# Samples' weight panels: eight head-free ones put into the heads, and twelve multiplied as high and low parts in place of plain f32

## What is computed

```python
proj = rmsnorm(x, g_norm) @ w_in
u_p, z_p, q, k, v, z_r, gates = split(proj)           # u_p, z_p: 1024; q, k: 4 x 256; v, z_r: 4 x 512; gates: 2 x 1024
gate_p, gate_r = split(gates + b_gate)
pooled = multi_scale_pool(u_p, pool_buf)              # windows 2, 4, 8, 16, then a 256 x 256 matrix a group, times pool_scale
y_pool = (pooled * silu(z_p)) @ w_branch_pool
o, s_new = retention(rope(q), rope(k), v, ret_state)  # per head; s_new = decay * s + k^T v
y_ret  = (norm(o) * gn_ret * silu(z_r)) @ w_branch_ret
merged = sigmoid(gate_p) * y_pool + sigmoid(gate_r) * y_ret
out = rmsnorm(x + merged @ w_out, g_final)
```

## Time and profile before

| | us |
|---|---|
| runs | 3106.29, 3093.57, 3103.41; median 3103.41 |
| the profiled execution | 3093.96 |
| its span | 3092.4 |
| TensorE busy | 2985.6 (97%) |
| VectorE busy | 1832.8 (59%) |
| ScalarE busy | 1153.4 (37%) |
| HBM traffic | 188 GB/s over the span |

### The profile page before, as it was taken

How to read it: one execution, slowest core, us unless ns; L and a number is a source line. 1 busy time by engine, 2 the same in 40 slices (tenths; PEclk the granted TensorE clock), 3 DMA queues, 4 the chain that set the end, 5 groups by cost and what they waited for, 6 DMA issues and landing times.

```text
span 3092.4 us, 36008 instructions
## 1 busy us (share of the span) xinstructions
PE 2985.6 (97%) x13000; PEld 2299.2 (74%) x13000; DVE 1832.8 (59%) x2590; ACT 1153.4 (37%) x1892; POOL 709.0 (23%) x503
## 2 busy tenths in 40 slices
PE   6999999999999999999998999999999999999997
PEld 5888888888778888888887878778888878762222
DVE  7666566765454757566664575667567466744331
ACT  5434444445554434443433233333333333322110
POOL 4253534343332344433432000000000000001110
PEclk9999999999999999999999999999999999999999
DMA  4535354435643444534446556635744673558885
GB/s 131 196 122 193 130 184 143 172 133 186 200 152 127 162 157 150 177 140 171 153 143 268 206 177 247 253 118 182 272 171 160 248 276 121 200 182 324 304 302 196
DMA packets 297599, 582.06 MB, mean 188 GB/s; under 512 B 24840, under 2 KB 167688, under 8 KB 286255
## 3 DMA queue, kind: packets, MB, share of 16 engines
q1 hardware_dynamic: 292039, 562.73, 51.4%
q0 software_dynamic: 5392, 17.12, 1.5%
HBM read 410.63 MB, written 169.50 MB: 188 GB/s over the span
## 4 chain that ended last, share of the span: by engine, by line
PE 86%; DVE 7%; issue 3%; DMA 2%; ACT 1%; POOL 1%; SPq 0%; DVEq 0%; ACTq 0%; POOLq 0%
PE bank L1160 25%; PE bank L1162 25%; PE bank L1161 25%; PE bank L1455 7%; PE bank L1493 2%; PE bank L1208 1%; DMA raw<-in_w_branch_pool 1%; DVE z_in L2163 1%; DVE win_a L1891 1%; DVE wa_lo L1891 1%; DVE z_lo L1891 1%; PE bank L1486 1%; DVE c_out L1891 1%; DVE xs L1905 1%; DVE stats L2143 0%
## 5 line engine op out<-in xcount | busy, mean ns | idle before, releaser
L1160 PE MATMUL bank<-xa_hi,wa_hi 128*128 128x512 f32 x2240 | 884.9, 395 | 12.3 <-DVE c_out L1891 8.1
L1162 PE MATMUL bank<-xa_hi,wa_lo 128*128 128x512 f32 x2240 | 874.6, 390 | 0.0
L1161 PE MATMUL bank<-xa_lo,wa_hi 128*128 128x512 f32 x2240 | 873.6, 390 | 0.0
L1160 PEld LDWEIGHTS bank<-xa_hi,wa_hi 128*128 128x128 f32 x2240 | 421.4, 188 | 100.5 <-issue 15.9
L1162 PEld LDWEIGHTS bank<-xa_hi,wa_lo 128*128 128x128 f32 x2240 | 421.3, 188 | 89.1
L1161 PEld LDWEIGHTS bank<-xa_lo,wa_hi 128*128 128x128 f32 x2240 | 421.8, 188 | 84.2
L1891 DVE TENSOR_TENSOR wa_lo<-w_raw,wa_hi 128x512 fp32r<-128x512 f32 x320 | 312.2, 978 | 192.2 <-ACT wa_hi L1591 191.0
L1891 DVE TENSOR_TENSOR wa_lo<-w_sum,wa_hi 128x512 fp32r<-128x512 f32 x240 | 195.1, 813 | 225.0 <-ACT wa_hi L1591 225.0
L1891 DVE TENSOR_TENSOR w_lo<-raw,w_hi 128x512 fp32r<-128x512 f32 (+1 forms) x288 | 180.5, 658 | 228.6 <-ACT w_hi L1699 228.5
L1591 ACT ACTIVATE wa_hi<-w_raw 128x512 fp32r<-128x512 f32 x320 | 200.8, 628 | 245.6 <-PE bank L1162 242.1
L1699 ACT ACTIVATE w_hi<-raw 128x512 fp32r<-128x512 f32 (+1 forms) x288 | 165.8, 603 | 279.7 <-PE bank L1162 106.5
(11 more groups left out here) (241 smaller groups left out, 4607.8 us busy)
## 6 DMA issues: line engine op xcount, KB each, us to landing
w_raw<-in_w_in SPq DMA_DIRECT2D x80, 1024.0 KB, 5.1
v_d<-turned SPq DMA_DIRECT2D x64, 512.0 KB, 3.2
qk_s<-qk_d SPq DMA_DIRECT2D x32, 1024.0 KB, 7.1
v_s<-v_d SPq DMA_DIRECT2D x32, 1024.0 KB, 11.1
raw<-in_w_branch_ret SPq DMA_DIRECT2D x128, 256.0 KB, 4.1
s_w<-in_w_in SPq DMA_DIRECT2D x64, 512.0 KB, 5.1
tabs<-in_c_rope SPq DMA_DIRECT2D x16, 1024.0 KB, 6.6
qk_d<-high SPq DMA_DIRECT2D x32, 512.0 KB, 4.4
```

The costliest lines, as they stand in the source:

```text
L1160: pe.matmul(out, lh, rh, start=first, stop=False, skip_group_check=onto)
L1161: pe.matmul(out, lh, rl, start=False, stop=False, skip_group_check=onto)
L1162: return pe.matmul(out, ll, rh, start=False, stop=last, skip_group_check=onto)
```

## The change

One table, `PANELS`, now numbers all panels of the samples in the order in which they are used. The head-free panels go into the heads: u0 and u1 into the first, zp0 and zp1 into the second, gp0 and gp1 into the third, gr0 and gr1 into the fourth, both right behind z; their sigmoids and products go with them. The pooling windows run at the end of the second head, the mixing matmuls ahead of the fourth head's transposes. The loops over heads are unrolled.

Twelve panels, z of each head and those eight, are multiplied in split form. ScalarE copies a pair to fp32r (`s_hi`, a ring of HRING = 4), VectorE subtracts that from the weights in place (`s_lo` lies over `s_w`), and TensorE does high x high, high x low and low x high for each k-tile. q/k, v, branch, mixing, pool-branch and output panels stay plain f32. SyncE loads the next head's states between the two head-free panels, each when the same sample's state has been scaled.

```diff
-PH = 16
-SQK, SV, SZ, SBR = 0, 4, 8, 12
-SU0, SU1, SZP0, SZP1, SGP0, SGP1, SGR0, SGR1, SMIX, SBP0, SBP1, SOUT0, SOUT1 = (
-    0, 4, 8, 12, 16, 20, 24, 28, 32, 36, 40, 44, 48)
+
+
+PANELS = []
+for _h, _others in enumerate((("u0", "u1"), ("zp0", "zp1"), ("gp0", "gp1"), ("gr0", "gr1"))):
+    PANELS += [("qk", _h), ("v", _h)] + [("mix", None)] * (_h == HEADS - 1) + [("z", _h)]
+    PANELS += [(name, None) for name in _others] + [("br", _h)]
+PANELS += [(name, None) for name in ("bp0", "bp1", "out0", "out1")]
+
+SPLIT = [panel for panel in PANELS if panel[0][0] in "zug"]
+HRING = 4
...
         s_w = at("s_w", [P, SRING, 2, 512])
+        place[0] = s_w_place
+        s_lo = at("s_lo", [P, SRING, 2, 512], F32R)
...
+        s_hi = at("s_hi", [P, HRING, 2, 512], F32R)
...
             for h in range(HEADS):
                 if h:
                     load_qkv(h)
-                sp.wait_ge(s_act.sem, s_act.done("head", h, None))
-                for q in seqs:
-                    src = io["state_ret"][0, q, h].rearrange("(k p) v -> p k v", p=P)
-                    sp.dma_start(s_in[:, q], src).then_inc(s_state_in[q], 16)
-                load_columns(h, SZ, COL_ZR)
+                if h == HEADS - 1:
+                    for k in range(4):
+                        load_pair(pair("mix", None, k), io["w_pool_group"][0, k], GW)
+                load_columns("z", h, h * DV + COL_ZR)
+                for p in range(2):
+                    name, first = (("u", COL_U), ("zp", COL_ZP), ("gp", COL_G), ("gr", COL_G + D))[h]
+                    load_columns(f"{name}{p}", None, first + 512 * p)
+                    if p == 0 and h + 1 < HEADS:
+                        load_states(h + 1, seqs)
...
+            def split_panel(name, h, bank):
+
+                out = banks[bank][0:S, :]
+                for k in range(KT):
+                    c = split_number(name, h, k // 2)
+                    m, a = split_pair(c), k % 2
+                    if a == 0:
+                        pe.wait_ge(s_lo_done, c + 1)
+                    w_high, w_low = s_hi[:, c % HRING, a, :], s_lo[:, m % SRING, a, :]
+                    pe.matmul(out, sx_hi[:, k, :], w_high, start=k == 0, stop=False)
+                    pe.matmul(out, sx_hi[:, k, :], w_low, start=False, stop=False)
+                    mm = pe.matmul(out, sx_lo[:, k, :], w_high, start=False, stop=k == KT - 1)
+                    if a:
+                        mm.then_inc(s_w_used, 1)
...
-                panel(h, SZ, 6, sx)
+                if h == 1:
+                    wait("head", h, "u_t")
+                if h == HEADS - 1:
+                    wait("head", h, "mix1")
+                if h == 0:
+                    wait("once", 0, "x_low")
+                split_panel("z", h, 6)
+
+                other = ("u", "zp", "gp", "gr")[h]
+                split_panel(f"{other}0", None, 2)
+                wait("head", h, "new7_1")
+                split_panel(f"{other}1", None, 0)
...
+            def highs_of(name, h):
+
+                for k in range(4):
+                    c = split_number(name, h, k)
+                    m = split_pair(c)
+                    act.wait_ge(s_w_in[m % SRING], 16 * loads(m))
+                    if c >= HRING:
+                        act.wait_ge(s_w_used, SRING + split_pair(c - HRING) + 1)
+                    act.activation(s_hi[:, c % HRING], s_w[:, m % SRING], ACT.Copy).then_inc(s_hi_done, 1)
...
                 for q in range(5):
                     scaled(h, q)
+                highs_of("z", h)
                 wait("head", h, "bias")
                 do(s_norm[:], banks[1][0:S, :], ACT.Identity, scale=s_small[:, 3:4], bias=s_small[:, 4:5])
                 for q in range(5, SB):
                     scaled(h, q)
-                used(h, SZ + 4)
+                other = ("u", "zp", "gp", "gr")[h]
+                highs_of(f"{other}0", None)
+                used("z", h)
                 do(s_og[:], banks[6][0:S, :], ACT.Sigmoid)
-            for k, bank in enumerate((0, 1)):
-                used(None, (SU0, SU1)[k] + 4)
-                do(s_u[:, k * 512:(k + 1) * 512], banks[bank][0:S, :])
-            for k, bank in enumerate((4, 5)):
-                used(None, (SZP0, SZP1)[k] + 4)
-                do(s_z[:, k * 512:(k + 1) * 512], banks[bank][0:S, :], ACT.Sigmoid)
-            for k in range(4):
-                wait("tail", 0, f"bias{k}")
-                do(s_g[:, k, :], s_g[:, k, :], ACT.Sigmoid)
-            wait("tail", 0, "pg_t", s_mm)
+                highs_of(f"{other}1", None)
...
+            def lows_of(name, h):
+
+                for k in range(4):
+                    c = split_number(name, h, k)
+                    m = split_pair(c)
+                    dve.wait_ge(s_hi_done, c + 1)
+                    tt(s_lo[:, m % SRING], s_w[:, m % SRING], s_hi[:, c % HRING].bitcast(F32), ALU.subtract, s_lo_done)
...
+                lows_of("z", h)
...
+                lows_of(("u", "zp", "gp", "gr")[h] + "0", None)
                 wait("head", h, "z_sig", s_act)
                 st(s_og[:], banks[6][0:S, :], s_og[:], ALU.mult)
                 wait("head", h, "z_silu")
                 st(s_og[:], s_norm[:], s_og[:], ALU.mult)
+                lows_of(("u", "zp", "gp", "gr")[h] + "1", None)
+                other(h, 0)
                 wait("head", h, "og_t", s_mm)
                 dve.wait_ge(s_norm_in, h * 16 + 16)
                 st(s_ogt[:], banks[6][:, 0:4 * S].rearrange("p (k t) -> p k t", t=S),
                    s_gn[:].rearrange("p (k o) -> p k o", o=1).broadcast_to([P, 4, S]), ALU.mult)
+                other(h, 1)
```

More of the change, by code:

```diff
@@ L496, in build, with pair, split_pair, split_number @@
+        def pair(name, h, k=0):
+            return 4 * PANELS.index((name, h)) + k
+        def split_pair(c):
+            return 4 * PANELS.index(SPLIT[c // 4]) + c % 4
+        def split_number(name, h, k):
+            return 4 * SPLIT.index((name, h)) + k
+        def loads(m):
+            return sum(2 if PANELS[i // 4][0] == "qk" else 1 for i in range(m % SRING, m + 1, SRING))
         w_in = io["w_in"][0]
@@ L1105, in _ @@
             pool.wait_ge(out_mm, KT * NB)
+            pool.wait_ge(s_mm.sem, s_mm.done("once", 0, "hist"))
             pool.memset(s_y[:], 0.0).then_inc(fills, 1)
@@ L1852, in scaled @@
                 do(s_out[:, q % 4], s_in[:, q], scale=s_decay[:, 0:1])
-            with act.Fori(0, HEADS) as h:
+            for h in range(HEADS):
                 wait("head", h, "rope5")
@@ new lines, in sample_mix @@
+            def sample_mix():
+                h = HEADS - 1
+                dve.wait_ge(s_gate_in, 32)
+                used("mix", None)
+                for p, bank in enumerate((3, 6)):
+                    w = slice(p * 512, (p + 1) * 512)
+                    st(s_mix[:, w], banks[bank][0:S, :], s_pool_s[:, w], ALU.mult)
+                for p in range(2):
+                    w = slice(p * 512, (p + 1) * 512)
+                    wait("head", h, f"mix{p}")
+                    st(s_mix[:, w], s_mix[:, w], s_z[:, w], ALU.mult)
@@ new lines, in other @@
+            def other(h, p):
+                w = slice(p * 512, (p + 1) * 512)
+                bank = banks[(2, 0)[p]][0:S, :]
+                if h == 1:
+                    wait("head", h, f"other{p}", s_act)
+                    st(s_z[:, w], bank, s_z[:, w], ALU.mult)
+                elif h > 1:
+                    dve.wait_ge(s_gate_in, 32)
+                    used(("gp", "gr")[h - 2] + str(p), None)
+                    st(s_g[:, 2 * h - 4 + p, :], bank, s_gate_b[:, 2 * h - 4 + p, :], ALU.add)
@@ L2371, in _ @@
+            for h in range(HEADS):
+                used("qk", h)
                 qk = banks[4][:].rearrange("p (s a f) -> p s a f", s=2, a=2)
@@ L2443, in _ @@
-            for g in range(GROUPS):
-                k = slice(2 * g, 2 * g + 2)
-                wait("tail", 0, f"window{GROUPS - 1}")
-                stt(s_pool[:, k], (s_wa, s_wb)[g % 2][:, k, :, 16:20], 1.0 / WINDOWS[g], s_ext[:, k, :, 16:20],
-                    ALU.mult, ALU.subtract)
+                if h == 1:
+                    sample_windows()
+            for p in range(2):
+                w = slice(p * 512, (p + 1) * 512)
+                wait("head", HEADS - 1, f"other{p}", s_act)
+                wait("tail", 0, None)
+                st(s_y[:, w], s_y[:, w], s_g[:, 2 + p, :], ALU.mult)
@@ L2461, in _ @@
[L2461 to L2471 removed]
+                used(f"bp{p}", None)
```

327 lines of the change are left out of this document (166 added, 161 removed).

## The result

The changed kernel takes 3104.15 us (median of 20 runs, 3097.93 to 3109.24), the kernel before, beside it on the same chip, 3096.11 us (20 runs, 3089.16 to 3109.62). The ratio is 1.0022, with a 95% interval of 1.0012 to 1.0032: +6.8 us (8.0 by the medians), small but told apart from nothing. By the bound of 0.5% that is "no change", as forecast. The forecast had +2.8 us, and 3106 us on the shown median of 3103.41. That 3106 lies within 2 us of 3104.15 is luck: the median of three runs was 7.3 us above that of twenty, and the change was forecast 4 to 5 us too cheap. The kernel before varies by 20 us from run to run, and its granted clock with it (0.992 in a run of 3090.48 us, 0.984 in one of 3109.9), so a difference of a few us between two profiled executions says little by itself. The profiled executions show +9.3 (3101.7 against 3092.4 of span).

The account below looks back on a forecast made before the run. TensorE, busy 2985.6 of 3092.4 us, was taken as the bound. Heads +61.8, kept tail work +4.2 and removed tail -63.2 gave +2.8 us, put onto the median of 3103.41: 3106 us, range 3094 to 3119.

Parts of the forecast that it names:

- no change: Whole kernel: a result within 0.5%, 15.5 us, of before; chance 62%, against slower 25% and faster 13%.
- A split panel: TensorE, z and the eight head-free panels: 5.55 us each as fp32r matmuls, against 7.00 plain.
- Rival 4: Split panels: fp32r is slow, 0.283 us a matmul; +6 us, 3112, inside the forecast, no separate chance.
- The rate of highs and lows: Per pair of k-tiles ScalarE needs 1.052 us, VectorE 1.221, less than TensorE's 1.39: no bound.
- The wait behind z: Every head, between z and the first head-free panel: TensorE idle 6.2 us, replacing a 3.2 us break.
- The second wait: Before the second head-free panel: TensorE waits 2.3 us for its weights in three heads, not in the fourth.
- The landing behind the states: Second head-free panel's first weight load: lands 8.3 us after issue, the middle of 5.1 and 11.6.
- The half clock: First head-free panel of each head, behind the wait after z: 1.3 us lost to half clock.
- The tail: After the fourth head's branch panels: 63.2 us go; 4.2 us of transposes and mixing matmuls stay, in heads 2 and 4.
- the bounds listed for the range: Whole kernel: the load landing's -7 and +10 us, and a clock lost not at all or twice, -4 and +8.
- the first (the clock decides): Sample heads: half clock after the waits makes the kernel slower, +18 us, 3124; chance 17%.
- Rival 3: Sample heads: highs and lows come in time, -35.5 us, 3068, or half of it, 3085; chance 13% for both.

Follow-up runs that it names:

- filled: split_own with 44 more fp32r matmuls, results unused, in every head between z and the first head-free panel; 3090.87 us, ratio 0.9977.
- z_plain_own_mix: z_plain_own with the fourth head's mixing weights loaded ahead of its states; 3070.87 us, ratio 0.9919.
- experiment 3: The changed kernel with z back to plain f32, the eight head-free panels still split and in the heads; 3094.51 us, ratio 0.9996.
- Experiment 1: The changed kernel with the next head's states loaded behind both head-free panels instead of between them; 3103.6 us, ratio 1.003.
- experiments 5 to 7: move_own, z_plain_own and split_own, in this order: each head loads its own states behind its q/k and v weights; 3079.7, 3081.13 and 3098.89 us.
- experiment 4: The changed kernel with all twelve split panels plain f32, the eight head-free ones still in the heads; 3086.36 us, ratio 0.9969.
- z_plain_own: experiment 3 with each head's own states loaded behind its q/k and v weights; 3081.13 us, ratio 0.9926.
- split_own: The changed kernel, all twelve panels split, with each head's own states loaded behind its q/k and v weights; 3098.89 us, ratio 1.0.
- move_own: experiment 4 with each head's own states loaded behind its q/k and v weights; 3079.7 us, ratio 0.9933.

## Why the prediction was right

The class, the sign and the mechanism held: the shorter products were paid for by waits that the queues' order makes, and the two nearly cancel. Step by step:

- **A split panel, 5.55 us.** 5.6 us measured, with 32 columns stationary as with 128. Rival 4, 0.283 us a matmul, falls: 0.233.
- **The rate of highs and lows.** 1047 and 1221 ns a pair, as the earlier trace rows; no bound in after. In filled and z_plain_own_mix it begins to be one.
- **The wait behind z, 6.2 us in each head.** 5.67, 5.70, 5.67 and 5.88 us, released by VectorE's s_lo, by the chain that was forecast: lows of z, statistics, bias, last scaled states, highs. Counted from z's start, the third head's first high of the next panel was to end at 2923.1 - 2912.5 = 10.6 us and TensorE to start at 11.8; it was 2959.77 - 2949.63 = 10.1 and 11.4. Experiments 3 and 6 confirm the cause: with z plain at most 0.4 us of the wait is left, in both orders of the loads.
- **The second wait, 2.3 us in three heads.** 3.42, 1.46 and 1.97 us, 6.9 in all, as forecast, and none in the fourth. The landing behind the states, taken as 8.3 us, was 10.80, 9.23 and 9.43 in the three heads. Experiment 1 confirms the cause: with the states behind both panels this wait is gone. It came back before the branch panels, whose loads now stood behind the states in the queue. What the forecast did not say is that the DMA engines themselves stand nearly idle for about 5 us in the second and third heads of after, while SyncE's queue waits for scaled states. With each head loading its own states (experiments 5 to 7) neither of these two waits is left, only one in the fourth head for the mixing weights. In after the DMA engines are full only from the issue on. A row of after, of that time:

```profile
2960.00:2961.00 1.00, 0.00 (x0) 0.00 (x0) 1.00 (x2) 1.00 (x2) 0.93 (x2) 0.50 1.13 424
```

  It shows 424 GB/s at a DMA share over 1, so a window this short is rough; one of 10 us in filled has 386 (last section). The figure of about 358 GB/s for a core (the Trainium skill, "DMA: Bandwidth & Descriptors", Specifications) is passed here as in the rows before; the measurement stands.
- **The half clock, 1.3 us in the first other panel.** This term of the sum was mis-sized: the forecast let half clock add 4 x 1.3 us and take away 3 x 1.28 + 2.57, -1.2 in all, and the sums above are 17.4 against 9.3, +8.1. From a first other panel's start to the start of the wait behind it, after needs 8.05, 8.44 and 8.12 us (first head: 2825.84 - 3.42 - 2814.37) for what z of the second head does in 5.74 at full clock (2877.22 to 2882.96): 2.3, 2.7 and 2.4 lost. The forecast had taken the price from the branch panels of the third head, where a break of 3.2 us lost 1.28; its own row for the fourth had 2.57. Three more falls were not in it, 1.7 us each: in the first head's second other panel (behind its wait of 3.42 us), in the third head's first states and in the output panels (15.63 against 13.93). Filled shows that the loss behind the wait belongs to TensorE's idleness; the others may be chance.
- **The tail, -63.2 us and 4.2 kept.** From the end of the fourth head's branch panels it is 3101.7 - (3051.21 + 7.0) = 43.5 us to the end, where before less the removed 63.2 would give 42.2. The 1.7 us of half clock in the output panels more than cover the difference.

The sum closes. To the start of the fourth branch panels the forecast had 17.4, 16.7, 16.1 and 18.3 us more than before for the four heads (with the 4.2 kept in the second and fourth and the half clock that goes with the third's branch), 68.5 in all. Measured are 20.4 (20.80 less the 0.4 by which the samples start later), 16.4, 17.8 and 18.8, 73.4 in all. 4.9 from the heads and 1.3 from the tail are 6.2 of the 6.5 us between +2.8 and +9.3. The first head alone is 3 over, with its second wait of 3.42 us and the fall in the panel behind it; the third is 1.7 over, with its first states at half clock. In two places the forecast's own arithmetic is off, and no term of the sum hangs on either: VectorE's four lows of the first other panel end at 2924.3 + 3 x 1.22 = 2928.0, not 2929.2, and the bounds listed for the range (-11 and +18) would give 3095 to 3124 if they came together, not 3094 to 3119.

Of the rivals, the first (the clock decides) was the nearest to what happened: right in kind, and the miss is a third of its size. The rule that came with it, that a wait which returns with each tile makes the next start cold each time (the Trainium skill, "TensorE: Matmul & The Clock Gate", HAM oscillation), is borne out by after: all four first other panels start at 0.63 us a matmul, and none does in filled. It does not hold for every wait that returns: behind those of 1.46 and 1.97 us the second other panel starts at 0.39. Rival 3 (the queues don't hold TensorE) was wrong for this kernel. The version nearest to it splits the eight panels, leaves z plain and puts the loads in another order: -25 us measured, against the -35.5 that it named, of which 4 x 1.45 = 5.8 were z's split. The move alone gave 23 of these 25.

What the forecast did not see is that the change is three changes with different signs. By the medians against before: the move alone is worth -8 us (experiment 4), the split of the eight panels adds 8 in this load order (experiment 3 against 4), and the split of z 8 more (after against 3), +8 in all. With each head loading its own states the three are -19, +1 and +18 (experiments 5 to 7; by the ratios the +1 is -2, so it isn't told from nothing), and with the mixing weights first the move is -23. For the move the forecast's own numbers were at hand: the break of 3.2 us becomes 1, with 1.3 to 2.6 us of half clock behind it, in four heads, and 2.5 us of s_mix are hidden, about 18 us.

What stays open: why the clock falls where TensorE had been busy (below), which happened three times in z_plain_own and never in z_plain_own_mix; and whether splitting the eight panels, 1.6 us a head by the chains, is worth anything in the medians. A deeper ring of highs, which would let the first other panel's highs be made together with z's, was not tried, nor was an order of VectorE that takes the norm's statistics ahead of a part of z's lows.

## What to carry to other kernels

Before giving a helper engine work to speed up the critical one, follow what stands behind that work in the helper's queue: here 4.5 us of lows ahead of a norm delayed scaled states, loads and the next panel, and made z's split cost 18 us net, though its products alone saved 6. Take a change that moves, splits and reorders apart before judging it: the move was worth 8 us, or 23 with better load order, and the whole came out at +6.8. Loads that wait for a buffer hold up every load behind them in their queue, and the DMA engines too: look for a place in the order where no reader behind them is near. Here that was behind the head's own q/k and v weights, and the kernel with the move alone went from 3086.4 to 3079.7 us by it.

## What the hardware showed unexpectedly

- Useless matmuls in a wait made a kernel faster: split_own's 1.0 [0.9984, 1.0015] became 0.9977 [0.9963, 0.9992], and their 12 runs each don't overlap.
- The clock also falls without a long break of TensorE. In filled TensorE was busy 28.9 of the 30 us before 2850, in three waits of 0.38, 0.37 and 0.34 us it lost the rest (the last two between the transposes and the states), and the clock was at half from 2851 on, for about 4 us. The falls at the states in after, move_own and z_plain_own stand at the same place; z_plain_own_mix has the same waits and no fall, so they alone don't make one:

```profile
2820.00:2830.00 10.00, 9.62 (x37) 3.78 (x38) 3.54 (x4) 2.04 (x3) 3.37 (x7) 1.00 1.02 264
2830.00:2840.00 10.00, 10.00 (x25) 3.66 (x24) 1.36 (x2) 0.00 (x0) 1.39 (x3) 1.00 1.08 367
2840.00:2850.00 10.00, 9.29 (x36) 4.18 (x34) 5.80 (x19) 1.82 (x4) 0.00 (x0) 1.00 1.05 386
...
2851.00:2852.00 1.00, 1.00 (x2) 0.18 (x1) 0.00 (x0) 0.00 (x0) 0.00 (x0) 0.50 1.06 393
...
2855.00:2865.00 10.00, 10.00 (x26) 2.62 (x24) 5.09 (x8) 3.45 (x3) 2.19 (x3) 1.00 0.89 337
```

- A matmul in fp32r of 512 moving columns takes the same 0.23 us with 32 columns stationary (after) as with 128, and a plain f32 one of the same size 0.875.
